# Four stages of a hybrid gMLP and state-space layer, from four blocks with barriers to one block

## The reference, cut to what matters

```python
h = rmsnorm(x) * (1 + sc1) + sh1
gate_a, gate_b, u, v, z, xbc, dt_f, dt_b = split(h @ w_in)
# gMLP: v is normed and mixed over the 128 tokens of a chunk, per group of 128 columns
y_a = gelu(u) * (einsum('gts,bcsgd->bctgd', ws, rmsnorm(gelu(v))) + bs)
branch_a = sigmoid(gate_a) * (y_a @ w_branch_a)
# input of the state-space mixer: five-tap depthwise convolution over tokens, then silu
xbc = silu(dwconv(xbc, conv_w) + conv_b)
dt = softplus([dt_f, dt_b] + dt_bias);  A = dt * -exp(a_log)
# and silu(z), sigmoid(gate_b), used by later stages
```

## Time and profile before

| | us |
|---|---|
| median of 3 runs | 1561.56 |
| lowest and highest | 1560.65, 1561.61 |
| the profiled execution | 1557.0 |
| its span in the profile | 1555.3 |
| TensorE busy | 1302.7 |
| VectorE busy | 835.1 |
| ScalarE busy | 668.5 |
| GpSimd busy | 263.5 |
| granted clock of TensorE, mean of the span | 0.919 |

### The profile page before, as it was taken

One profiled execution on the slowest core, in us unless ns is written; L12 is line 12 of the kernel. 1 busy time (PEld: TensorE's weight loads), 2 busy tenths in 40 slices (PEclk: granted clock), 3 DMA queues, 4 the chain that ended last, 5 costly groups with the idle time before them and its releaser, 6 DMA issues. The chain is left out here.

```text
span 1555.3 us, 20614 instructions
## 1 busy us (share of the span) xinstructions
PE 1302.7 (84%) x7887; PEld 1154.1 (74%) x7887; DVE 835.1 (54%) x972; ACT 668.5 (43%) x1031; POOL 263.5 (17%) x285
## 2 busy tenths in 40 slices
PE   3999989799998999947788844999880799999970
PEld 1789989799997888944566643999770688888860
DVE  2411442277665111105778759333464499999966
ACT  2423330144443222127567737111140477777743
POOL 0600000000000010025599861000002000000002
PEclk9999999999999999978899966999985899999995
DMA  9992112112212243154466541331645599999935
GB/s 385 412 363 71 66 38 99 37 55 82 70 67 82 90 148 123 52 185 142 149 190 196 199 153 78 115 107 64 259 162 194 195 397 405 421 403 413 413 154 203
DMA packets 62497, 289.09 MB, mean 186 GB/s; under 512 B 9104, under 2 KB 13648, under 8 KB 42064
## 3 DMA queue, kind: packets, MB, share of 16 engines
q1 hardware_dynamic: 49424, 242.19, 42.0%
q0 software_dynamic: 12608, 45.62, 7.5%
q10 hardware_dynamic: 384, 0.16, 0.0%
HBM read 239.51 MB, written 48.43 MB: 185 GB/s over the span
## 5 line engine op out<-in xcount | busy, mean ns | idle before, releaser
L212 PE MATMUL banks<-rounded,rounded 128*128 128x320 f32 (+1 forms) x1168 | 366.1, 313 | 20.2 <-DVE rounded L735 6.9
L213 PE MATMUL banks<-rounded,rounded 128*128 128x320 f32 (+1 forms) x1168 | 363.9, 312 | 0.0
L214 PE MATMUL banks<-rounded,rounded 128*128 128x320 f32 (+1 forms) x1168 | 363.7, 311 | 0.0
L191 DVE TENSOR_TENSOR rounded<-words,rounded 128x2048 fp32r<-128x2048 f32 x52 | 119.2, 2292 | 225.7 <-ACT rounded L183 223.4
L1916 DVE TENSOR_TENSOR rounded<-words,rounded 128x2048 fp32r<-128x2048 f32 x96 | 219.7, 2290 | 32.9 <-ACT rounded L1907 32.0
L212 PEld LDWEIGHTS banks<-rounded,rounded 128*128 128x128 f32 (+1 forms) x1168 | 220.8, 189 | 21.5 <-issue 13.9
L213 PEld LDWEIGHTS banks<-rounded,rounded 128*128 128x128 f32 (+1 forms) x1168 | 220.9, 189 | 0.3
L214 PEld LDWEIGHTS banks<-rounded,rounded 128*128 128x128 f32 (+1 forms) x1168 | 220.6, 189 | 0.3
L1907 ACT ACTIVATE rounded<-words 128x2048 fp32r<-128x2048 f32 x96 | 183.9, 1916 | 47.1 <-PE banks L2032 39.4
L183 ACT ACTIVATE rounded<-words 128x2048 fp32r<-128x2048 f32 x52 | 99.3, 1909 | 138.0 <-PE banks L233 62.8
L1191 ACT ACTIVATE words<-words,words 128x128 f32<-128x128 f32 x320 | 97.7, 388 | 62.0 <-DMA words<-decay_sums 62.0
(11 more groups left out here) (269 smaller groups left out, 1971.7 us busy)
## 6 DMA issues: line engine op xcount, KB each, us to landing
words<-in_units SPq DMA_DIRECT2D x52, 1024.0 KB, 5.0
words<-in_wg SPq DMA_DIRECT2D x32, 1024.0 KB, 7.4
words<-in_wu SPq DMA_DIRECT2D x32, 1024.0 KB, 7.7
words<-in_wd SPq DMA_DIRECT2D x32, 1024.0 KB, 8.2
words<-decay_sums SPq DMA_DIRECT2D x40, 512.0 KB, 3.8
words<-in_w_mod_rest SPq DMA_DIRECT2D x32, 512.0 KB, 4.3
slot_rows<-words POOLq DMA_DIRECT2D x27, 512.0 KB, 24.1
expert_rows<-words POOLq DMA_DIRECT2D x25, 512.0 KB, 9.1
```

The lines of the kernel that those rows point to most:

```text
L191: self.nc.vector.tensor_tensor(self.lo[:, i % 2, :], self.raw[:, i % 2, :], self.hi[:, i % 2, :].bitcast(F32), ALU.subtract).then_inc(self ...
L212: nc.tensor.matmul(out, lhs[0](k), rhs[0](k), start=(k == 0), stop=False)
L213: nc.tensor.matmul(out, lhs[0](k), rhs[1](k), start=False, stop=False)
L214: last = nc.tensor.matmul(out, lhs[1](k), rhs[0](k), start=False, stop=(k == nk - 1))
```

## The change

The four stages no longer open a block each. Each collects its five programs in an object, and `build` opens one block in which every engine runs its four programs one after the other. `stage_ssd` keeps its own block. Where a barrier had kept things apart, waits or other places take over:

```diff
+class Programs:      # keeps one program for each engine: sp, pe, act, dve, pool
 def build(nc, io, out):
-        ya = stage_gmlp(kit, stream, io, scr)
-        stage_branch_a(kit, stream, ya)
-        stage_conv(kit, stream, io)
-        stage_gates(kit, stream, scr)
+        steps = StepWeights(kit, io)
+        gmlp, ya, gate_done, hi_done, lo_done, mixed, zeroed = stage_gmlp(kit, stream, io, scr)
+        branch_a, merged = stage_branch_a(kit, stream, ya, gate_done, hi_done, lo_done, mixed, steps)
+        conv, tiles_taken, turns_taken = stage_conv(kit, stream, io, steps, merged, zeroed)
+        gates = stage_gates(kit, stream, scr, tiles_taken, turns_taken)
+        with nc.Block() as block:
+            @block.tensor
+            def _(pe):
+                gmlp.pe(pe)
+                branch_a.pe(pe)
+                conv.pe(pe)
+                gates.pe(pe)
...
 # stage_gmlp, POOL
-            pool.wait_ge(s_zo, 16 * len(rows))
 # stage_branch_a, SyncE: the step sizes' weights (raw, bias, alog) now go to O_X
+            if i == 2:
+                sp.wait_ge(mixed, KD)
+                dt.load(sp)
 # stage_branch_a, TensorE
+                else:
+                    pe.wait_ge(gate_done, 7 + t)
+                if i == 0 and t == 0:
+                    last = first_tile(pe)
...
+        def first_tile(pe):
+            wh, wl = (v[:, :, 0:P] for v in w.parts(0, KD))
+            for h in range(2):
...
+                for k in range(KD):
+                    if h == 0:
+                        pe.wait_ge(ya_hi_done, k + 1)
+                        pe.wait_ge(*ya_lo_done(k))
...
 # stage_branch_a, ScalarE and VectorE
             w.split_hi(act, i + 1)
+            if i == 1:
+                dt.split_hi(act)
...
+        dve.wait_ge(gate_done, KD)
             w.split_lo(dve, i + 1)
+            if i == 1:
+                dt.split_lo(dve)
 # stage_conv, TensorE
-            pe.wait_ge(d_hl, 2)
+        pe.wait_ge(weights.split, 2)
...
-                last = split3(nc, ps[0:64, h, 0:HALF], ...
+            last = split3(nc, ps[0:64, 4 + h, 0:HALF], ...
         last.then_inc(d_pe, 1)
+        w.ready(pe, 0)
+        pe.wait_ge(merged, 7)
+        feature_tile(nc, w.parts(0, KD), 0, ht, lambda h: halves(kit, 0)[:, h, :], KD).then_inc(s_t0, 1)
         pe.wait_ge(d_act, 1)
         for c in range(NC):
-                last = nc.tensor.transpose(ps[:, 2, ...
+            last = nc.tensor.transpose(ps[:, 6, ...
         last.then_inc(d_pe, 1)
         for i in range(n):
             w.ready(pe, i)
             for t in range(2):
                 if i:
                     pe.wait_ge(s_pre, 3 * (2 * i + t - 1))
                 elif t:
-                        pe.wait_ge(d_act, 3)
+                    pe.wait_ge(merged, 8)
+                else:
+                    continue
...
+            if i == 1:
+                pe.wait_ge(d_act, 3)
 # stage_conv, ScalarE and VectorE: lines 686 and 735 are gone from here
+        dve.wait_ge(*zeroed)
 # stage_gates, TensorE
                 if half == 0 and m >= 8:
                     pe.wait_ge(s_silu, m - 7)
+                elif i == 0 and c == 0:
+                    pe.wait_ge(*turns_taken)
+                elif i == 0 and c == 4:
+                    pe.wait_ge(*tiles_taken)
-                    last = token_part(nc, w.parts(i, 4), c, half, ht, ps[:, (1 + m) % 8, :])
+                last = token_part(nc, w.parts(i, 4), c, half, ht, ps[:, (4 + m) % 8, :])
...
-                        pe.wait_ge(s_silu, NC * (nz // 2 - 1) + 2 * t + 2)
+                    pe.wait_ge(s_silu, NC * nz // 2 - 8 + 2 * t + 2)
```

More of the change, by code:

```diff
@@ L129, in sync, with __init__, tensor, scalar @@
         self.eng.wait_ge(self.sem, self.n)
+class Programs:
+    def __init__(self):
+        self.sp = self.pe = self.act = self.dve = self.pool = None
+    def sync(self, program):
+        self.sp = program
+    def tensor(self, program):
+        self.pe = program
+    def scalar(self, program):
+        self.act = program
+    def vector(self, program):
+        self.dve = program
+    def gpsimd(self, program):
+        self.pool = program
 class Weights:
@@ new lines, in _ @@
+    @block.scalar
+    def _(act):
+        for i in range(4):
+            w.split_hi(act, i + 1)
+            if i == 1:
+                dt.split_hi(act)
+    @block.vector
+    def _(dve):
+        dve.wait_ge(gate_done, KD)
+        for i in range(4):
+            w.split_lo(dve, i + 1)
+            if i == 1:
+                dt.split_lo(dve)
+            for t in range(2):
+                dve.wait_ge(*(w.done(i) if t else (s_t0, i + 1)))
+                tile = MG[:, 2 * i + t, :]
+                nc.vector.tensor_tensor(two(tile), halves(kit, t), two(tile), ALU.mult).then_inc(s_mg, 1)
@@ L609, in stage_conv @@
+    return block, s_mg
+def stage_conv(kit, stream, io, weights, merged, zeroed):
     nc, ps = kit.nc, kit.ps
@@ new lines, in stage_gates, with _ @@
+    block = Programs()
+    @block.sync
+    def _(sp):
+        for i in w.to_load():
+            w.load(sp, i)
+    @block.tensor
+    def _(pe):
+        for i in range(nz):
+            w.ready(pe, i)
+            n, half = divmod(i, 2)
+            for c in range(NC):
+                m = NC * n + c
+                if half == 0 and m >= 8:
+                    pe.wait_ge(s_silu, m - 7)
+                elif i == 0 and c == 0:
[3 more added lines that the diff above has]
+                last = token_part(nc, w.parts(i, 4), c, half, ht, ps[:, (4 + m) % 8, :])
+                if half and c < NC - 1:
+                    last.then_inc(s_pe, 1)
+            last.then_inc(w.used, 1)
+        for i in range(nz, nz + ng):
+            w.ready(pe, i)
+            for t in range(2):
+                if i > nz:
+                    pe.wait_ge(s_sig, 2 * (i - nz - 1) + t + 1)
+                else:
+                    pe.wait_ge(s_silu, NC * nz // 2 - 8 + 2 * t + 2)
+                last = feature_tile(nc, w.parts(i, KD), t, ht, lambda h: halves(kit, t)[:, h, :], KD)
+                if t == 0:
+                    last.then_inc(s_t0, 1)
+            last.then_inc(w.used, 1)
@@ new lines, in _ @@
+    @block.scalar
+    def _(act):
+        for n in range(nz // 2):
+            w.split_hi(act, 2 * n + 1)
+            w.split_hi(act, 2 * n + 2)
+            for c in range(NC):
+                act.wait_ge(*((s_pe, (NC - 1) * n + c + 1) if c < NC - 1 else w.done(2 * n + 1)))
+                if n:
+                    act.wait_ge(s_out[c], 16 * n)
+                nc.scalar.activation(zs[:, c, :], ps[:, (4 + NC * n + c) % 8, :], ACT.Silu).then_inc(s_silu, 1)
+        for i in range(nz, nz + ng):
+            if w.exists(i + 1):
+                w.split_hi(act, i + 1)
+            for t in range(2):
+                act.wait_ge(*((s_t0, i + 1 - nz) if t == 0 else w.done(i)))
+                if i > nz:
+                    act.wait_ge(s_gout[t], 16 * (i - nz))
+                nc.scalar.activation(two(gs[:, t, :]), halves(kit, t), ACT.Sigmoid).then_inc(s_sig, 1)
```

951 lines of the change are left out of this document (467 added, 484 removed).

## The result

| | before | after |
|---|---|---|
| median of 4 runs each, us | 1561.11 | 1545.64 |
| lowest and highest | 1560.24, 1561.61 | 1541.0, 1548.42 |
| ratio after to before, 95% interval | | 0.9911 [0.9892, 0.993] |
| the profiled execution | 1557.0 | 1545.03 |
| its span | 1555.3 | 1543.3 |

The account below looks back on a forecast made before the run. TensorE was taken to set the first four stages' time, so only waits between its matmuls count. Boundary gains 5.1 + 2.5 + 8.4 = 16.0 us took 1561.56 to 1545.6; range 1541.0 to 1551.0.

Parts of the forecast that it names:

- First boundary: gMLP to branch: TensorE does 21 matmuls while VectorE finishes group 7, gaining 5.1 us; bounds 0.7 and 5.6.
- The 22nd matmul's wait: In the branch's first tile, TensorE waits some 0.6 us for VectorE's group 7, without losing the clock.
- Second boundary: Branch to step sizes: weights prepared beside the branch's matmuls, gaining 2.5 us net of a longer wait for unit 17.
- The wait for unit 17: In the convolution, TensorE's wait for its second unit grows from 2.58 to about 9.8 us.
- the chain behind the transposes: Convolution: transposes, softplus series, memsets and unit 17's splits, 17.38 us to that unit's first matmul, taken as unchanged.
- the bound of 12.4: Second boundary: upper bound of the gain, if unit 17 did not wait for the chain at all.
- Third boundary: Convolution to gates: the gates need neither tile 23's taps nor its silu, so TensorE goes on without a gap, gaining 8.4 us.
- The lower bound: Third boundary: the least gain, 0.3 us, if only the barrier itself is saved.
- Rival 1: All three boundaries: only the barriers' own price comes back, TensorE waiting for the same data; 2.1 us, 1559.5; chance 4%.
- Rival 2: Convolution: the 9.8 us wait for unit 17 and its ramp don't appear; 27.4 us gained, 1534.2; chance 4%.
- Rival 3: Unit 17 through gates: the clock falls to half beyond 167.6 us without a gap; costs 142 us, 1688; chance 3%.
- zeroed: Convolution's wait for the zero stores costs nothing: the last is issued at 62.8 and lands at most 49.7 us later.

Follow-up runs that it names:

- branch_waits: The changed kernel, but TensorE waits for all eight groups of the gMLP's result before the branch's first matmul; 1550.55 us, ratio 0.9918 to the kernel before.
- late_steps: The changed kernel, but the step sizes' weights are loaded and split after the branch's last product, as before the change; 1554.51 us, ratio 0.9948.
- turn_first: The changed kernel, but TensorE turns the step sizes before the convolution's tile (0, 0), not behind it; 1538.91 us, ratio 0.9879 to the kernel before.
- spread: The changed kernel, but unit 17's splits and the memsets precede the step sizes' chain, VectorE's 16 series steps spread behind units 17 to 20's taps; 1531.36 us.
- gates_wait: The changed kernel, but the gates' first matmul waits for the convolution's last silu (tile 23); 1551.2 us, ratio 0.9938 to the kernel before.
- zeros_paired: The changed kernel, but the 37 zero stores are made as 19 with the same bytes; 1542.12 us, ratio 0.9904 to the kernel before.
- drain_zeros: The changed kernel, but POOL drains once behind the zero stores, beside the gMLP; 1541.89 us, ratio 0.9894 to the kernel before.
- spread_drain: spread with two POOL drains added, behind the zero stores and behind the gates' last store but one; 1525.56 us, ratio 0.9797 to the kernel before.

## Why the prediction was right, and where it was not

- **First boundary.** 5.1 us were forecast, 5.0 came (8.98 to 3.98). (The forecast had 0.08 us for VectorE's signal, where its rows, 322.49 to 322.59, give 0.10.) The 22nd matmul's wait is 0.63 us, in the range of 0.5 to 0.7. The products run on at the full step: the next is at 233.01, and from there on they are 0.15 us apart. `branch_waits` shows that the waits by group are what pays.
- **Second boundary.** 2.5 us were forecast, 2.3 came (69.80 to 67.49). The move of the loads to the branch's time is what pays (`late_steps`), and the moved work is covered there. ScalarE's rounding of those weights is one line in the kernel after,

```profile
245.94 0.61 ACT L608 ACTIVATE rounded<-words 128x512 fp32r<-128x512 f32 x1
```

  some 40 us ahead of TensorE's need. The wait for unit 17 grew to 9.6 us, with 9.8 forecast (its terms, 17.38 - 0.45 - 7.04, give 9.89; the tile beside the chain took 7.3 us to the end of its last matmul, where 7.04 was put; the bound of 12.4 is 2.47 + 9.89, the terms printed beside it give 12.3), and the chain behind the transposes kept its 17.38 us (17.37). `turn_first` and `spread` show what it hangs on.
- **Third boundary.** 8.4 us were forecast. The gates' ninth matmul comes 1.84 us after their first, and the stage's part of the table gives 6.84 + 1.64 = 8.5. The lower bound is printed as 0.3, where its own working gives 0.45; nothing hangs on it.
- **The three barriers.** I priced them at 0.45 to 0.69 us each. `branch_waits`, `gates_wait` and `late_steps` bring back 6.0, 8.1 and 9.3 us with no barrier in them, so most of each boundary was its data waits, as forecast. Rival 1 falls by this, and by the timeline of the change, where the waits at the second and third boundary are gone and 0.63 us are left of the first.
- **Rival 2** said that unit 17 isn't late. It is, by the 9.61 us in the timeline. `spread`, built to make rival 2 true, takes 24.1 us less than the kernel before from the last mixing to the scan; the rival's 27.4 less the 3.0 lost at the scan's barrier would be 24.4.
- **Rival 3**, that the full clock doesn't last, falls twice. The stretches of the kernel after from 322 to 650 us show it:

```profile
322.00:485.00 163.00, 163.00 (x1139) 162.91 (x1138) 114.09 (x121) 69.77 (x138) 0.00 (x0) 1.00 0.21 72
485.00:650.00 165.00, 165.00 (x865) 146.27 (x864) 29.31 (x16) 41.21 (x46) 14.58 (x27) 1.00 0.30 104
```

  That is 328 us of work without a gap at 1.00, and in `spread` 410 us. The Trainium skill (TensorE: Matmul & The Clock Gate, Seeing it yourself) has a peak-current limit that wants a third busy core on the die. One core is busy here and no fall was seen under load, so these traces agree with it and don't test it.

**The step that failed** is this one: "`stage_ssd` still begins behind a barrier, so what the first four stages gain passes on whole, and nothing behind it changes", and with it the mark "the start of `stage_ssd` 16 us earlier". The three boundaries gain 15.8 us, with 16.0 forecast. At the barrier 3.0 are lost again. The scan's first matmul comes 13.3 us earlier, counted from the gMLP's first. (In the clock of the span it is 670.14 - 659.75 = 10.4 us, because this execution began the gMLP 2.9 us later.) I had looked at the barrier as a point in time. It is also a place where POOL's drain stands, and the change removed the earlier, covered place. The rows were there: the events of line 296 of the kernel before have the drain of 3.085 us, 118 us ahead of its barrier. I costed `zeroed` at nothing by the landing of the stores, which is right for the data and leaves out the drain.

The median met the forecast to 0.04 us all the same. That is partly luck. By the sections the effect is 12.8 us, which is 1561.56 - 12.8 = 1548.8, inside the range. The forecast's terms without the drain's 3.0 come to 13.0. The comparisons give 12.6 to 16.7 us, with intervals 6 to 10 us wide. Whether the part behind the scan's start is truly a little faster (883.6, 884.1 and 882.8 us in the three profiles of the change, 885.2 in the one of before) stays open: one profile of before can't tell.

## What to carry to other kernels

A barrier between two stages costs little by itself (under 0.7 us here) and much by what it makes wait: read for each boundary which data the next stage's first instructions need, and let them wait for that piece by piece. When blocks are merged, follow every engine to the barrier that remains: what it drained early and unseen before, it now drains there, and POOL's drain grew by 0.08 us with each plain DMA that it had issued since its last drain, in the four stages studied here. And once the gaps are closed, look at what was behind the new largest wait: here the chain of the step sizes was worth 11.5 us more, the drains 5.2.

## What the runs showed of the hardware

**In the first four stages POOL's drain goes by the number of its DMAs.** POOL's drains in the first four stages of five of the kernels, with the DMAs that it issued since the drain before:

```
kernel         at us     DMAs  drain us
before        112.62      37    3.085
before        667.52      28    2.345
after         654.08      65    5.382
zeros_paired  651.40      47    3.907
drain_zeros   112.69      37    3.090
drain_zeros   654.34      28    2.340
spread_drain  112.32      37    3.086
spread_drain  634.30      27    2.263
spread_drain  641.60       1    0.119
```

A line through the drains behind 1 and 65 DMAs, 0.119 + 0.0822 for each further DMA, gives 2.34 at 28, 3.08 at 37, 3.90 at 47 and 5.38 at 65: within about 0.01 us all through. It would give 0.037 at none, and POOL's drains in the blocks of the branch and the convolution of the kernel before, with no DMA issued, took 0.040 and 0.034. The stores had landed before each drain began, so it isn't a wait for data. What the engine does in it no run here shows. In later stages it doesn't hold: in the kernel before the drains there are 1.29 us after 25 DMAs (10 of them indirect), 14.1 us after 4 indirect ones, and up to 18.9 us after none.

**The barrier's own walk is shorter than I priced it.** By the walk I mean the time from the end of the last engine's drain to TensorE's first matmul. In the kernel after POOL's drain ends at 654.08 + 5.38 = 659.46 and TensorE starts at 659.75: 0.29 us. In the kernel before it is 669.86 to 670.14, 0.28. At the end of the gMLP in the kernel before VectorE came last: its work ended at 230.25, its drain of 0.017 us began at 230.50, and TensorE started at 230.94, 0.42 us behind it. So my 0.69 us took in 0.27 us of VectorE's way into the barrier. The Trainium skill (Runtime: NRT & Kernel Launch, The ~15µs preamble/postamble breakdown) has about 355 ns for the walk of the sync barrier ahead of a kernel. These walks, at a block's end, lie on both sides of it.

**The slow start after a stand isn't one number.** The loss against full rate was 1.4 us after the 4.24 us stand, 1.6 after 6.65 and 1.6 after 2.58 in the kernel before, 1.6 again after 9.61 in the kernel after, and 2.7 in `branch_waits` after 3.94. It doesn't follow the length of the stand. In a sum it has to be given a range of more than a microsecond, and I had given it a microsecond.
